# All high products of a unit ahead of all its low products, on TensorE

## What is computed

```python
def swiglu(x, w_gu, w_down):
    gate, up = jnp.split(x @ w_gu, 2, axis=-1)
    return (jax.nn.silu(gate) * up) @ w_down

for l in range(DEPTH):
    h = h + 0.5 * swiglu(rms_norm(h, p['norm_ffn1'][l]), p['ffn1_w_gu'][l], p['ffn1_w_down'][l])
    u = rms_norm(h, p['norm_mix'][l])
    m = mixer_ab(u, ...) if l % 2 == 0 else mixer_c(u, ...)   # Mamba-2 and GLA heads; HGRN2 heads
    h = h + m
    h = h + 0.5 * swiglu(rms_norm(h, p['norm_ffn2'][l]), p['ffn2_w_gu'][l], p['ffn2_w_down'][l])
y = rms_norm(h, p['norm_final'])
```

## Time and profile before

| | us |
|---|---|
| median of 3 runs | 2327.61 |
| lowest, highest | 2326.52, 2328.1 |
| the profiled execution | 2327.2 |
| its span, first to last instruction | 2325.5 |
| TensorE busy | 2294.0 |
| VectorE busy | 1720.5 |
| ScalarE busy | 1143.9 |

### The profile page before, as it was taken

One profiled execution on the slowest core, in us unless ns is written; L12 is line 12 of the kernel. 1 busy time (PEld: TensorE's weight loads), 2 busy tenths in 40 slices (PEclk: granted clock), 3 DMA queues, 4 the chain that ended last, 5 costly groups with the idle time before them and its releaser, 6 DMA issues.

```text
span 2325.5 us, 49874 instructions
## 1 busy us (share of the span) xinstructions
PE 2294.0 (99%) x20579; PEld 2266.2 (97%) x20579; DVE 1720.5 (74%) x2587; ACT 1143.9 (49%) x1769; POOL 14.4 (1%) x50
## 2 busy tenths in 40 slices
PE   8999999999999999999999999999999999999998
PEld 8999999999999999999999999999999999999998
DVE  7767876788577567677867767876888867767885
ACT  6434444676354545343445434444677756424453
POOL 1000000000000000000000000000000000000000
PEclk9999999999999999999999999999999999999999
DMA  4323333332422223333323323332222223323331
GB/s 149 105 77 103 94 96 86 94 119 74 121 71 63 76 82 93 98 92 106 95 82 98 111 75 103 95 94 84 70 71 68 69 74 91 96 82 102 88 107 57
DMA packets 397773, 209.92 MB, mean 90 GB/s; under 512 B 11679, under 2 KB 393750, under 8 KB 397558
## 3 DMA queue, kind: packets, MB, share of 16 engines
q1 hardware_dynamic: 392166, 203.17, 30.7%
q10 hardware_dynamic: 5392, 3.72, 0.5%
HBM read 201.41 MB, written 5.45 MB: 89 GB/s over the span
## 4 chain that ended last, share of the span: by engine, by line
PE 83%; DVE 7%; ACT 4%; DVEq 3%; issue 1%; ACTq 1%; DMA 0%; SPq 0%
PE PD L2509 8%; PE PM L2619 8%; PE PM L2617 8%; PE PD L2514 8%; PE PM L2618 8%; PE PD L2515 8%; PE PD L2513 7%; PE PD L2510 7%; PE PD L2516 7%; PE PD L2619 3%; PE PD L2617 3%; PE PD L2618 3%; DVE wlo L1488 1%; DVE c_xl L2199 1%; DVE c_xl L2175 1%
## 5 line engine op out<-in xcount | busy, mean ns | idle before, releaser
L653 ACT ACTIVATE whi<-raw 128x1024 fp32r<-128x1024 f32 (+3 forms) x231 | 229.1, 992 | 356.7 <-PE PD L2516 350.8
L1488 DVE TENSOR_TENSOR wlo<-raw,whi 128x1024 fp32r<-128x1024 f32 (+3 forms) x233 | 267.3, 1147 | 69.3 <-ACT whi L653 47.9
L2509 PE MATMUL PD<-XB,whi 128*128 128x288 f32 x856 | 262.8, 307 | 2.2 <-DVE wlo L1488 2.0
L2514 PE MATMUL PD<-XB,whi 128*128 128x288 f32 x856 | 252.8, 295 | 0.0
L2515 PE MATMUL PD<-XB,wlo 128*128 128x288 f32 x856 | 252.0, 294 | 0.0
L2513 PE MATMUL PD<-XB,whi 128*128 128x256 f32 x856 | 241.9, 283 | 0.3 <-DVE XB L1526 0.3
L2510 PE MATMUL PD<-XB,whi 128*128 128x256 f32 x856 | 240.0, 280 | 0.0
L2516 PE MATMUL PD<-XB,wlo 128*128 128x256 f32 x856 | 238.3, 278 | 0.0
L2619 PE MATMUL PM<-XT,WL 128*128 128x272 f32 x720 | 208.3, 289 | 0.0
L2617 PE MATMUL PM<-XT,WH 128*128 128x272 f32 x720 | 207.6, 288 | 0.0
L2619 PE MATMUL PM<-XB,WL 128*128 128x272 f32 x720 | 207.6, 288 | 0.0
(11 more groups left out here) (519 smaller groups left out, 6683.7 us busy)
## 6 DMA issues: line engine op xcount, KB each, us to landing
raw<-in_ffn_w_down SPq DMA_DIRECT2D x64, 512.0 KB, 3.8
V<-in_ffn_w_gu SPq DMA_DIRECT2D x60, 512.0 KB, 3.9
V<-in_ffn_w_gu SPq DMA_DIRECT2D x120, 256.0 KB, 4.5
raw<-in_ab_w_in SPq DMA_DIRECT2D x44, 512.0 KB, 3.9
raw<-in_ffn_w_gu SPq DMA_DIRECT2D x32, 512.0 KB, 3.8
raw<-in_c_w_in SPq DMA_DIRECT2D x32, 512.0 KB, 4.0
raw<-in_ffn_w_down SPq DMA_DIRECT2D x32, 384.0 KB, 3.3
VF<-in_ffn_w_gu SPq DMA_DIRECT2D x12, 512.0 KB, 4.6
```

Source lines behind the costliest of these rows:

```text
L653: A(high_of(ps)[:, 0:k, :], raw[ps % 4][:, 0:k, :], ACT.Copy).then_inc(S["hi_ready"], 1)
L1488: TT(low_of(u)[:, 0:k, :], raw[u % 4][:, 0:k, :], high_of(u)[:, 0:k, :].bitcast(F), ALU.subtract).then_inc(S["lo_ready"], 1)
L2509: mm(front, hi, x[:, 0, r, 0:FRONT], start=first, stop=False)
L2514: mm(front, hi, x[:, 1, r, 0:FRONT], start=False, stop=False)
```

## The change

In `unit`, `unit_rows` and `half_unit` the four high products of every row are issued first, then the two low products of every row. The wait for `lo_ready`, which stood at the head of a unit, now stands between the two; at the head stands a wait for `hi_ready`. The row-by-row waits for activations stay with the high products. A piece of a unit (`unit_rows` with some rows) is regrouped within itself. Nothing is changed on the other engines.

```diff
-            def row_products(ps, r, x, first, final, before=None):
+            def high_products(ps, r, x, first, before=None):
...
                 mm(front, hi, x[:, 1, r, 0:FRONT], start=False, stop=False)
-                mm(front, lo, x[:, 0, r, 0:FRONT], start=False, stop=final)
-                return mm(rest, lo, x[:, 0, r, FRONT:T], start=False, stop=final)
+
+            def low_products(ps, r, x, final):
+
+                out = line(ps)
+                lo = low_of(ps)[:, r, :]
+                mm(out[:, 0:FRONT], lo, x[:, 0, r, 0:FRONT], start=False, stop=final)
+                return mm(out[:, FRONT:T], lo, x[:, 0, r, FRONT:T], start=False, stop=final)
...
             def unit_rows(ps, r0, r1, k, x, before=None):
 
                 if r0 == 0:
-                    pe.wait_ge(S["lo_ready"], ps + 1 + CREDIT)
+                    pe.wait_ge(S["hi_ready"], ps + 1)
                     pe.wait_ge(S["pair_read"], ps - 1 + CREDIT)
                 for r in range(r0, r1):
-                    last = row_products(ps, r, x, r == 0, r == k - 1, before and (lambda p: before(p, r)))
+                    high_products(ps, r, x, r == 0, before and (lambda p: before(p, r)))
+                if r0 == 0:
+                    pe.wait_ge(S["lo_ready"], ps + 1 + CREDIT)
+                for r in range(r0, r1):
+                    last = low_products(ps, r, x, r == k - 1)
```

More of the change, by code:

```diff
@@ L2500, in _ @@
             mm = pe.matmul
-            def row_products(ps, r, x, first, final, before=None):
+            def high_products(ps, r, x, first, before=None):
                 out = line(ps)
                 front, rest = out[:, 0:FRONT], out[:, FRONT:T]
-                hi, lo = high_of(ps)[:, r, :], low_of(ps)[:, r, :]
+                hi = high_of(ps)[:, r, :]
                 if before:
@@ L2514, in row_products @@
                 mm(front, hi, x[:, 1, r, 0:FRONT], start=False, stop=False)
-                mm(front, lo, x[:, 0, r, 0:FRONT], start=False, stop=final)
-                return mm(rest, lo, x[:, 0, r, FRONT:T], start=False, stop=final)
-            def unit(ps, i, k, x, before=None, order=None):
+            def low_products(ps, r, x, final):
[3 more added lines that the diff above has]
+                return mm(out[:, FRONT:T], lo, x[:, 0, r, FRONT:T], start=False, stop=final)
+            def unit(ps, i, k, x, before=None, order=None):
+                rows = list(order or range(k))
+                hold("pe", S["hi_ready"], 2 * i + (ps + 1))
+                hold("pe", S["pair_read"], 2 * i + (ps - 1 + CREDIT))
+                for q, r in enumerate(rows):
+                    high_products(ps, r, x, q == 0, before and (lambda p: before(p, q)))
                 hold("pe", S["lo_ready"], 2 * i + (ps + 1 + CREDIT))
-                hold("pe", S["pair_read"], 2 * i + (ps - 1 + CREDIT))
-                for q, r in enumerate(order or range(k)):
-                    last = row_products(ps, r, x, q == 0, q == k - 1, before and (lambda p: before(p, q)))
+                for q, r in enumerate(rows):
+                    last = low_products(ps, r, x, q == k - 1)
                 last.then_inc(S["unit_done"], 1)
@@ L2586, in half_unit @@
                 u = end_unit + m
-                pe.wait_ge(S["lo_ready"], u + 1 + CREDIT)
+                pe.wait_ge(S["hi_ready"], u + 1)
                 pe.wait_ge(S["pair_read"], end_unit + t - 1 + CREDIT)
                 for r in range(KT):
-                    hi, lo = high_of(u)[:, r, :], low_of(u)[:, r, :]
+                    hi = high_of(u)[:, r, :]
                     mm(line_of(t), hi, AB[:, 0, r, t0:t1], start=r == 0, stop=False)
                     mm(line_of(t), hi, AB[:, 1, r, t0:t1], start=False, stop=False)
-                    last = mm(line_of(t), lo, AB[:, 0, r, t0:t1], start=False, stop=r == KT - 1)
+                pe.wait_ge(S["lo_ready"], u + 1 + CREDIT)
+                for r in range(KT):
+                    last = mm(line_of(t), low_of(u)[:, r, :], AB[:, 0, r, t0:t1], start=False, stop=r == KT - 1)
                 last.then_inc(S["unit_done"], 1)
```

## The result

The changed kernel takes 2330.76 us (median of 22 runs, 2328.7 to 2334.17) beside 2327.38 us of the kernel before on the same chip (22 runs, 2325.35 to 2329.21). The ratio is 1.0018 with a 95% interval of 1.0012 to 1.0024.

What follows compares the result with a forecast made beforehand. TensorE's product count and spacing were taken as the bound, with gains limited near 5 us. Terms 3.0 + 1.1 - 1.1 - 0.6 - 0.1 = +2.3, taken as +2.2 on 2327.6, gave 2329.8 us; range 2327.0 to 2332.8 (8 in 10).

Steps and rivals of the forecast that it cites:

- middle groups: First down unit of six-row groups, four times: low products deferred behind the last row cost 0.74 us each, +3.0 us.
- GOB: First output-projection unit reading GOB: sixteen low products run behind the last of four chained rows, +1.1 us.
- eight-row groups: First down units of groups of eight rows: no cost, with a margin of only 0.2 us.
- c_open: Third unit there starts when its high weights are ready, not its low ones: -1.1 us, and it stays.
- c_rest: First two rows there no longer stall on low weights: -0.6 us, and it stays.
- ffn1's start: First units of ffn1: some 2.0 us gained, then lost waiting for ScalarE's copy and VectorE's XB: 0.
- the last ffn: First unit ends some 1.7 us later, absorbed by the wait for the sum of squares, about 0.4 to spare.
- y projection: Its second unit starts earlier: about -0.1 us.
- spacing: Distance between dense products over 1707 rows: taken as 0, bounds -1 and +2.6 us.
- The clock: Rival: new stall near 68 us halves TensorE's clock, +1.7 us, 2331.5 alone; clock or spacing slower than 2332.3: 0.14.
- the middle wait breaks the density: Rival: each of 233 units pays a 0.1 us refill at its mid-unit wait, +23 us, 2353; chance 0.04.
- the gains are kept while the losses stay small: Faster rival: gains at start and heads stay (-2.0, -0.8), four small units lose less: around 2327; chance 0.14.

Runs made afterwards that it cites:

- e1: Changed kernel, but units that wait row by row for activations keep the old product order: 2325.95 us, ratio 0.9998 to the kernel before.
- e2: Kernel before, with the new order only in units that wait row by row for activations: 2330.64 us, ratio 1.0020 to the kernel before.
- e7: Changed kernel, but in units waiting for rows the last row's six products stay together behind all others: 2328.67 us, ratio 1.0004 to the kernel before.
- e5: Kernel before, regrouped only in the first up phase of the first ffn: 2329.21 us in one execution, only its trace read.
- its repetition: The changed kernel run again without edit, beside variants: 2331.19 us, ratio 1.0020 to the kernel before.
- e3: Changed kernel with the low-weight wait back at each unit's head, new product order kept: 2333.69 us, ratio 1.0032 to the kernel before.
- e4: Kernel before, regrouped with the mid-unit wait only in eight units whose low weights come late: 2324.19 us, ratio 0.9986.
- e6: Changed kernel with low products in snake order, front and rest swapped in every other row: 2330.82 us in one execution.

## Why the prediction came out as it did

**Right in mechanism and size: work out of its cover.** The middle groups were put at 0.74 each and cost 0.75 to 0.80; e1 takes the cost away, e2 brings it alone, e7 removes it by moving one row. GOB was put at 1.1 and cost 1.12. Of the chain of reasoning each link is seen: the operands come at the same time, the third product of the last row waits to the same point, and the deferred products follow. The eight-row groups with their margin of 0.2 us lost nothing, as forecast.

**Right: the early starts that stay.** c_open -1.09 for -1.1 and c_rest -0.67 for -0.6. One detail was named wrong. The prediction said that the c_open unit would start at the end of the high weights. Of ScalarE's two operations at 1895.13 the first, of 0.96 us, makes this unit's high weights, so they are ready at 1896.09. The trace names VectorE's queue after L2393, the reading of the output line two units back, as the releaser of the start at 1897.32; that reading ends at 1897.14. In the kernel before the two conditions fell together, the reading at 1891.03 and the high weights at 1891.32, which is why the size was right; it was luck that the prediction did not need to know which of them ends last. Most of the 1.5 us that TensorE still idles there can't be had from the weights.

**Right: absorbed gains.** ffn1's start (a wait of 1.15 us in its place, confirmed alone by e5) and the last ffn (the idle moved from the sum of squares to the row).

**A little small: the y projection.** -0.1 was put, -0.20 measured. With its first unit in the old order it is -0.73, so the new order gives away 0.5 us in the first unit, a loss for YB of the same kind as AB's, which the prediction netted without naming: the wait for YB at L2513 grew from 0.8 us in the trace before to 1.4.

**The term that was mis-sized: spacing.** The prediction took 0 between bounds of -1 and +2.6, on the ground that no pattern in view differed from another. Measured +1.8 us. Of it 0.28 lies in the stretch at 229, where the trace before happens to have the faster pace. Behind it, outside the places of the table, the small steps sum to 1.5, 1.6, 1.5, 1.8 and 1.5 us in the change, its repetition, e1, e3 and e7, and to +0.3, -0.3 and -0.6 in e2, e4 and e5, which have the old order nearly everywhere. The five agree in every part, the largest 0.5 to 0.6 between 603 and 818 and 0.3 between 257 and 565. So the order's share is 1.2 to 2.1 us, by which of the old order's traces one compares with. The medians agree: e4 is 3.1 us faster than the kernel before and e1 0.4, although e1 has the same early starts; the 2.7 between them is a little more, but each has an interval of 2 us to either side. Per product it is small: 1.2 us over 10242 products (1707 rows of six) is 0.12 ns. The ground given for the 0 was wrong: the patterns do differ. For the down units the prediction had the sign in its hands, twelve low products at 0.126 us where a mixed stretch gave 0.125, and rounded it away; that the old order had a faster pace elsewhere it had not looked for. Why the new order never reached that pace stays open; e6 shows that the change of part between neighbours explains the 0.04 us per six down units and nothing of the loss in the heads.

**The clock.** A stay of the granted clock at 1.2 GHz, brought by the new stall near 71 us or shifted by the one at 1941, was a rival on the slower side. The new stall brought none. Windows after (length, busy PE, PEld, DVE, ACT, POOL, clock, DMA share, GB/s):

```profile
585.20:588.60 3.40, 3.40 (x15) 2.90 (x14) 1.57 (x3) 1.37 (x2) 0.00 (x0) 0.50 0.52 153
1945.30:1948.70 3.40, 3.26 (x24) 3.04 (x24) 3.16 (x4) 1.93 (x3) 0.00 (x0) 1.00 0.24 67
```

The drop near 584 is there in both kernels; the one at 1945 is missing. That need not come from the change. A stretch of e5, whose code there is the old one, and the same stretch of e4:

```profile
1894.80:1898.20 3.40, 3.40 (x17) 3.40 (x17) 2.69 (x5) 0.00 (x0) 0.00 (x0) 0.50 0.31 96
```

```profile
1894.80:1898.20 3.40, 3.40 (x29) 3.40 (x29) 2.25 (x4) 0.95 (x1) 0.00 (x0) 1.00 0.20 58
```

e5 has a drop at 1895 and none at 1945, with the code of the kernel before. e2 and e3 have none near 584. So a drop comes or goes with the execution, each worth some 1.5 us amid dense work, where the prediction put 1.7 (steps of -1.53 where it is missing at 583, +1.54 where e5 has it). The times say it too, for one and the same code: the 28 runs of the kernel before beside e1 have mean granted clocks of 0.997 to 0.999, and medians of 2327.2 (11 runs at 0.997), 2326.2 (15 at 0.998) and 2324.7 (2 at 0.999). The table's -0.22 in the c heads and -0.90 after 1945 come again in e5 (-0.21 and -0.92), where the code is the old one; they belong to the profiled execution before. Leave these and the start out, and the steps of the change sum to 4.1 - 1.15 + 1.1 = 4.05 us, near the medians' 3.4 and 4.8. That the usual execution before is faster than the profiled one by this 1.1 is argued from such agreement (e1 comes to -0.8 beside -0.4 measured, e4 to -2.8 beside -3.1), not shown. So the sum of 2.2 was short by the spacing, and nearly by that alone. That the forecast of 2329.8 is only 1 us off although its sum is 1.8 short is in part luck: in the 22 runs the medians lie 3.4 apart, less than the steps, and the kernel before came out 0.2 below the median that the forecast started from.

**The other rivals.** That the middle wait breaks the density is refuted by the distances from L2514 to L2520: in the change none of the 307 is above 0.16 us and their mean is 0.132, and in e3, which has no middle wait, it is 0.132 too. The Trainium skill (TensorE: Matmul & The Clock Gate, LDWEIGHTS) has a price for an exposed load; no load became exposed at the 233 middle waits. That the gains are kept while the losses stay small, the faster side, fails with e2: the losses are 4.2 us.

## What to carry to other kernels

Reordering inside a unit has a price where the unit waits for late operands: count the work that stands behind the last one, before and after, for every deferred piece runs uncovered once that operand lands. Take the early start only where the postponed operand is the late one; here eight units of 233 gave 3.1 us where all of them lost 4. Where operands come in a chain, as for GOB, keeping the last one's products back is not enough; what is already possible has to run between them.

## What the runs showed of the hardware

- Dense products that follow row by row have two paces in the same code: 26.88 or 27.12 us for six units of 36 products, 124.4 or 125.6 ns each, in a whole stretch. With the low products behind all high ones there is one, 27.16, in twenty stretches of five traces. A difference of 1% in one stretch of one trace is no evidence for an order; the same stretch in several traces is.
- The halving of the granted clock for 3.4 us comes and goes too, at places that had idle time shortly before, each time 1.5 us where the work is dense. A stall of 1.15 us at 71 and of 1.5 at 1897 brought none.
- A wait in mid-stream that is already met costs nothing that can be read: 0.13 us from product to product, as without it.
